# Feed-forward 1: two conditioning sums per turn instead of three groups, the output gate's group in the last turns, and mixer 1's transfers and cast moved around the loop

## What is computed

```python
def swiglu(x, w_gate, w_up, w_down):
    return (jax.nn.silu(x @ w_gate) * (x @ w_up)) @ w_down      # feed-forward 1: 1024 -> 2816 -> 1024

# block 2, the conditioning of the layer:
mod  = jnp.split(jax.nn.silu(c)     @ w_mod[l] + b_mod[l], N_MOD, axis=-1)   # six parts of 1024
modc = jnp.split(jax.nn.silu(c_ctx) @ w_mod[l] + b_mod[l], N_MOD, axis=-1)
```

## Time and profile before

| | |
|---|---|
| median of 3 runs | 1234.78 us |
| lowest, highest | 1228.0, 1242.36 us |
| the profiled execution, its own time | 1236.44 us |
| its span in the trace | 1234.8 us |
| granted TensorE clock, mean share of full | 0.988 |
| busy: PE, DVE, ACT, POOL | 1182.5, 840.1, 633.5, 554.2 us |

### The profile page before, as it was taken

How to read it: one execution, slowest core, us unless ns; L and a number is a source line. 1 busy time by engine, 2 the same in 40 slices (tenths; PEclk the granted TensorE clock), 3 DMA queues, 4 the chain that set the end, 5 groups by cost and what they waited for, 6 DMA issues and landing times.

```text
span 1234.8 us, 24412 instructions
## 1 busy us (share of the span) xinstructions
PE 1182.5 (96%) x9128; PEld 1109.5 (90%) x9128; DVE 840.1 (68%) x1133; ACT 633.5 (51%) x1014; POOL 554.2 (45%) x287
## 2 busy tenths in 40 slices
PE   6999998999999999999999999997999999999998
PEld 6999998987788999999999888886877899999998
DVE  6798985955986577777554852688745696655555
ACT  5434445525762454454445546467426635655553
POOL 0355646832555433443435645468630383232331
PEclk9999998999999999999989999999999999999999
DMA  8777774443334557788614333232323354656563
GB/s 314 234 274 280 268 233 152 138 135 118 105 105 137 170 188 256 276 287 288 190 48 153 114 100 130 86 104 85 103 69 104 92 181 137 188 188 190 188 193 107
DMA packets 58096, 207.04 MB, mean 168 GB/s; under 512 B 6576, under 2 KB 8240, under 8 KB 57776
## 3 DMA queue, kind: packets, MB, share of 16 engines
q1 hardware_dynamic: 49824, 177.23, 43.9%
q0 software_dynamic: 6912, 25.17, 5.7%
q10 hardware_dynamic: 1296, 3.74, 0.9%
HBM read 205.07 MB, written 1.05 MB: 167 GB/s over the span
## 4 chain that ended last, share of the span: by engine, by line
PE 62%; DVE 19%; issue 6%; ACT 5%; POOL 4%; DMA 3%; DVEq 0%; SPq 0%; POOLq 0%; ACTq 0%
PE psum L639 17%; PE psum L640 17%; PE psum L641 16%; DVE parts L2160 4%; DMA low<-stream 3%; POOL own_parts L2907 2%; POOL high L2990 2%; DVE high L2191 1%; PE psum L931 1%; PE psum L650 1%; PE psum L652 1%; ACT parts L1498 1%; PE psum L651 1%; PE psum L778 1%; ACT parts L1567 1%
## 5 line engine op out<-in xcount | busy, mean ns | idle before, releaser
L639 PE MATMUL psum<-parts 128*128 128x256 f32 x1584 | 442.8, 280 | 20.0 <-DVE parts L2160 10.0
L640 PE MATMUL psum<-parts 128*128 128x256 f32 x1584 | 445.5, 281 | 0.0
L641 PE MATMUL psum<-parts 128*128 128x256 f32 x1584 | 441.7, 279 | 0.0
L2915 POOL TENSOR_TENSOR parts<-low,parts 128x1024 fp32r<-128x1024 f32 x60 | 169.9, 2832 | 337.8 <-ACT parts L1498 337.8
L639 PEld LDWEIGHTS psum<-parts 128*128 128x128 f32 x1584 | 299.5, 189 | 23.3 <-issue 18.0
L640 PEld LDWEIGHTS psum<-parts 128*128 128x128 f32 x1584 | 299.5, 189 | 0.0
L641 PEld LDWEIGHTS psum<-parts 128*128 128x128 f32 x1584 | 299.4, 189 | 0.0
L1498 ACT ACTIVATE parts<-low 128x1024 fp32r<-128x1024 f32 x198 | 205.4, 1054 | 124.2 <-DMA low<-stream 123.4
L2907 POOL TENSOR_TENSOR own_parts<-low,parts 128x1024 fp32r<-128x1024 f32 x75 | 184.0, 2465 | 161.2 <-ACT parts L1567 161.1
L2160 DVE TENSOR_TENSOR parts<-low,parts 128x1024 fp32r<-128x1024 f32 x138 | 179.0, 1331 | 22.0 <-ACT parts L1498 21.3
L640 PE MATMUL psum<-u_parts,parts 128*128 128x256 f32 (+1 forms) x560 | 164.0, 293 | 0.0
(11 more groups left out here) (377 smaller groups left out, 2083.8 us busy)
## 6 DMA issues: line engine op xcount, KB each, us to landing
low<-stream SPq DMA_DIRECT2D x334, 512.0 KB, 3.5
high<-conditioning POOLq DMA_DIRECT2D x48, 512.0 KB, 5.2
high<-wuq ACTq DMA_DIRECT2D x1, 1152.0 KB, 11.4
low<-x SPq DMA_DIRECT2D x4, 256.0 KB, 5.9
high<-ctx ACTq DMA_DIRECT2D x1, 1024.0 KB, 6.5
out<-low SPq DMA_DIRECT2D x8, 128.0 KB, 1.8
low<-cst ACTq DMA_DIRECT2D x1, 850.5 KB, 5.6
low<-vec ACTq DMA_DIRECT2D x1, 157.5 KB, 5.8
```

The lines of the kernel that those rows point to most:

```text
L639: pe.matmul(out, w_hi[:, cols_], x_hi, start=start, stop=False, **kw)
L640: pe.matmul(out, w_hi[:, cols_], x_lo, start=False, stop=False, **kw)
L641: return pe.matmul(out, w_lo[:, cols_], x_hi, start=False, stop=stop, **kw)
L2915: pool.tensor_tensor(ring_lo[k][:, j % RING, :], ring[:, t % RING, :], ring_hi[:, j % RING, :], ALU.subtract).then_inc(S("lower_ready_2"), 1)
```

## The change

- `COND_TURN[0]` falls from 5 to 4: the loop of feed-forward 1 sums groups 0 and 1 only, each for `c` and `c_ctx`: two sums in par 0, two in par 1. POOL loads two tiles in each turn, no longer three.
- The eight sums of group 2 (`gate_sums`, m = 0 to 7) come in the ninth turn, three per par, and two more between chunk 20 and chunk 21. Each stands behind hidden's lower part and, in the ninth turn, ahead of the two `lower` of its par. Their tiles go in turn through all three places, by `gate_sum_place`: m=0 to place 2 (loaded ahead of the loop), 1 to 0, 2 to 1, 3 to 2, and so on.
- POOL issues the loads of m=1 and m=2 in the eighth turn behind its `lower` of each par, m=3, 4, 5 in the ninth turn behind `lower` of par 0 (tile 62), m=6 and 7 behind that of par 1 (tile 65); each waits for the sum that frees its place.
- The first tiles of groups 0 and 1 and of m=0 are no longer loaded at once, but behind POOL's `lower` of tiles 8 (group 0) and 11 (group 1, m=0).
- ACT's five transfers move from before the norm's root to behind the two written-out chunks (behind `upper` of tile 11), ahead of the loop.
- DVE's wait for tables and the cast move behind feed-forward 1.
- The second feed-forward keeps its order; its tile counts follow from `COND_LOADS`.

Constants and the place of each tile:

```diff
-COND_TURN = (5, 3)
+COND_TURN = (4, 3)
 COND_FROM = (5, 5 + DC * 5 + 3)
-COND_DONE = tuple(a + DC * b for a, b in zip(COND_FROM, COND_TURN))
+COND_DONE = (5 + DC * 5, COND_FROM[1] + DC * 3)
+COND_TAIL = COND_FROM[0] + DC * 4
+COND_LOADS = (DC + 3, DC + 2, 3)
+def gate_sum_place(m):
+    g = (m + 2) % 3
+    return g, (DC, DC, 0)[g] + (m - (1, 2, 0)[g]) // 3 + 1
```

ACT:

```diff
+            def mixer_1_transfers():
+                act.dma_start(cst[:, P:NCST], dram["cst"][:, P:NCST]).then_inc(S("tables_loaded"), 16)
+                act.dma_start(lam_p, dram["lam"].partition_broadcast(P)).then_inc(S("tables_loaded"), 16)
+                act.dma_start(pos_i, dram["pos"].partition_broadcast(P)).then_inc(S("tables_loaded"), 16)
+                act.dma_start(wuq, dram["wuq"]).then_inc(S("small_weights"), 16)
+                act.dma_start(A1("wkr", 8), dram["wkr"]).then_inc(S("small_weights"), 16)
...
                     upper(k, 8 + 3 * par)
+                if k == 0:
+                    mixer_1_transfers()
                 with act.Fori(0, DC) as i:
...
             uppers(0, 2, RING)
-            act.dma_start(cst[:, P:NCST], dram["cst"][:, P:NCST]).then_inc(S("tables_loaded"), 16)
...
             take_root("ffn1_pre", D)
```

DVE:

```diff
-                    for g in ((0,), (1, 2))[par]:
+                    for g in (((0,), (1,)) if k == 0 else ((0,), (1, 2)))[par]:
...
+                def gate_sums(first, last):
+                    for m in range(first, last):
+                        g, load = gate_sum_place(m)
+                        dve.wait_ge(S(f"cond_tile{g}"), 16 * load)
+                        dve.wait_ge(S("cond_steps"), COND_TAIL + m)
+                        dve.scalar_tensor_tensor(out=cond_sums[2], in0=cond_places[g], scalar=small[:, 2 * m:2 * m + 1],
+                                                 in1=cond_sums[2], op0=ALU.mult, op1=ALU.add).then_inc(S("cond_steps"), 1)
...
-                    turn(DC, lambda i, par: None)
+                    turn(DC, (lambda i, par: gate_sums(3 * par, 3 * par + 3)) if k == 0 else (lambda i, par: None))
...
                     lower_hidden(k, par, FC * k + FC - 2 + par)
+                    if k == 0 and par == 0:
+                        gate_sums(6, 8)
...
+            dve.wait_ge(S("cond_ready"), 1)
+            ffn(0)
             dve.wait_ge(S("tables_loaded"), 48)
             link(dve.tensor_copy(posf, pos_i))
-            dve.wait_ge(S("cond_ready"), 1)
-            ffn(0)
```

POOL:

```diff
-                after = (2, 4, 5) if k == 0 else (1, 2, 3)
-                if k < 2:
+                after = (2, 4) if k == 0 else (1, 2, 3)
+                def gate_tile(m):
+                    g, load = gate_sum_place(m)
+                    pool.dma_start(cond_places[g], dram["conditioning"][3 * m + 2]).then_inc(S(f"cond_tile{g}"), 16)
+                def first_tile(g):
+                    pool.dma_start(cond_places[g], dram["conditioning"][3 * DC * k + g]).then_inc(S(f"cond_tile{g}"), 16)
+                if k == 1:
                     for g in range(3):
+                        first_tile(g)
                 for par in range(2):
                     lower(k, 8 + 3 * par)
+                    if k == 0:
+                        if par == 0:
+                            first_tile(0)
+                        else:
+                            first_tile(1)
+                            gate_tile(0)
...
                     for i in (DC - 1, DC):
                         for par in range(2):
                             lower(k, 14 + 3 * par, i)
+                            if k == 0 and i < DC:
+                                pool.wait_ge(S("cond_steps"), COND_TAIL - 2 + 2 * par)
+                                gate_tile(1 + par)
+                            elif k == 0:
+                                for m in ((3, 4, 5), (6, 7))[par]:
+                                    pool.wait_ge(S("cond_steps"), COND_TAIL + m - 2)
+                                    gate_tile(m)
```

More of the change, by code:

```diff
@@ L2185, in condition @@
                     beside(i, par)
-                    for g in ((0,), (1, 2))[par]:
-                        dve.wait_ge(S(f"cond_tile{g}"), i * 16 + (16 * DC * k + 16))
+                    for g in (((0,), (1,)) if k == 0 else ((0,), (1, 2)))[par]:
+                        dve.wait_ge(S(f"cond_tile{g}"), i * 16 + (16 * COND_LOADS[g] * k + 16))
                         dve.wait_ge(S("cond_steps"), i * COND_TURN[k] + COND_FROM[k])
@@ L2918, in feed_forward @@
             def feed_forward(k):
-                after = (2, 4, 5) if k == 0 else (1, 2, 3)
-                if k < 2:
+                after = (2, 4) if k == 0 else (1, 2, 3)
[5 more added lines that the diff above has]
+                if k == 1:
                     for g in range(3):
-                        pool.dma_start(cond_places[g], dram["conditioning"][3 * DC * k + g]).then_inc(S(f"cond_tile{g}"), 16)
+                        first_tile(g)
                 for par in range(2):
                     lower(k, 8 + 3 * par)
+                    if k == 0:
[4 more added lines that the diff above has]
+                            gate_tile(0)
                 if k < 2:
```

## The result

The changed kernel is slower: 1246.96 us in the median of 11 runs (1242.56 to 1255.2), the kernel before 1234.82 in as many beside it (1228.0 to 1242.36). The ratio is 1.0100, with a 95% interval of 1.0076 to 1.0125: some 12 us, where 2.8 us less were forecast. The profiled execution took 1249.6 us, of which 1247.6 are span.

A forecast was written before the change was run, and what follows sets the result against it. It took PE, busy 96% of the span, as the bound, with DVE pacing feed-forward 1's loop. 1234.8 - 2.7 (early part) - 4.8 (loop) + 4.7 (tail) = 1232.0 us, range 1225 to 1241.

The forecast's parts named there:

- Cast, and the first two gaps: Start of feed-forward 1: moving cast and transfers shrinks PE's gaps near 25 and 36 us, winning 1.4 and 1.8 us.
- The flood's new place: Transfers and first tile loads moved to some 34 to 46 us: a new cost of 0.5 us, from nothing to 1.8.
- The loop: Feed-forward 1's loop: one sum less brings DVE's turn from 17.42 to 16.22 us, PE sets the pace, 4.8 us won.
- The argument that feed-forward 2 has nearly as much DVE work: Said against the rival that a second 2.2 us collision per turn keeps the loop at 17.4 us; 1236.8 us, chance 0.10.
- The tail: Last two and a half turns of feed-forward 1: eight sums and their loads cost 4.7 us, between 3.5 and 5.9.
- The three gaps: New PE gaps in the tail, before up(21), down(20) and down(21): 3.5 to 6 us together, the last most certain.
- the lower clock of down(21): Rival: PE's clock falls in the tail's gaps, 48 matmuls at 0.1 us more, 4.8 us; 1236.8 us, chance 0.05.
- The floor of 2.0 us: End of the tail: even with the fastest landing, 3.9 us, PE loses at least 2.0 us before down(21).
- late loads: Rival: three tail loads at once land in 10 us rather than 4.6, about 9.5 to 10 us lost; 1237.3, chance 0.15.
- The range's upper end: Top of the median's range: cases lie between 1229.3 and 1237.3 us, and a median moves by some 4 us by itself.

The follow-up runs named there:

- e1: Kernel before with ACT's five transfers behind tile 11's upper part and the cast behind feed-forward 1, sums and loads as before; 1237.07 us, ratio 1.0024.
- e7: Kernel before with the cast behind feed-forward 1 and ACT's five transfers in the ninth turn, five sums per turn; 1234.19 us, ratio 0.9986.
- e8: Kernel before with only the wait for tables and the cast moved behind feed-forward 1; 1236.33 us, ratio 1.0019.
- e9: Kernel before with the cast behind feed-forward 1 and ACT's transfers inside the loop, five sums per turn; 1233.70 us, ratio 0.9981.
- e10: Changed kernel without the gate group's eight sums and loads, ACT's transfers inside the loop; 1233.13 us, ratio 0.9976 to the kernel before.
- e11: Changed kernel, whole, with only ACT's transfers moved inside the loop; 1245.23 us, ratio 1.0092 to the kernel before.
- e5: Changed kernel where POOL begins its subtractions for mixer 1's first weights only when all conditioning sums are done; 1249.95 us, ratio 1.0089 to the kernel before.
- e4: Changed kernel where all eight gate sums read the first tile and the other seven are not loaded; 1240.77 us, ratio 1.0048 to the kernel before.
- e6: Changed kernel with the last two gate sums behind the last chunk's product and lower part; 1247.22 us, ratio 1.0083 to the kernel before.
- e13: Changed kernel with the gate tiles' loads kept but without the eight sums; 1238.38 us, ratio 1.0023 to the kernel before.

## Why the prediction was wrong, point by point

- *Cast, and the first two gaps:* right. The first product ran at 22.18 (22.0 forecast), 3.2 us were won (3.2 before the flood's cost).
- *The flood's new place:* wrong, the second largest miss. The step put down 0.5 us, with 1.8 as its end; the trace has 5.6, 4.0 of gap and 1.6 of lower clock. It had the landing right (10.2, measured 10.8), and it looked at each tile's own way to PE. What it left out is ACT's order: the silu of one chunk stands behind the upper part of a tile of a later one, so a tile that PE wants only later holds up a hidden part that PE wants now. The early part as a whole thus lost 2.4 instead of winning 2.7.
- *The loop:* the size was near, 3.8 us for 4.8, in these two executions; the reason was wrong. "DVE sets the pace of this loop" was read from one execution that ran in the pattern of collisions. e1, e7 and e8 run five sums at PE's pace or within 1% of it, and e9 against e10 gives the fifth sum 0.6 us, within the noise. The 2.2 us of collision in the earlier trace rows were taken as a fixed part of DVE's turn; the traces tie the slow pace to them. (The argument that feed-forward 2 has nearly as much DVE work was weak: by the earlier trace rows it has 12.5 us per turn, where 14.4 are left here.)
- *The tail:* the step that failed most. The three gaps that it named came where it said, before up(21), down(20) and down(21), and two more. The sum was 4.7 us, at most 5.9; the trace has 13.9, and e11 against e10 gives 12.1. Missing were, first, the collisions: the text allowed one, of tile 62; there were four, of 8.5 us together, two of them with POOL's subtractions for mixer 1, which were not in the working at all. Then the lower clock of down(21), 2.5 us, which had a chance of 0.05. The floor of 2.0 us for the last gap was far too low for this trace (6.8); it is no floor either, since e5 has 1.6 there.
- *The rival "late loads"* (10 us lost) comes nearest in size, but its condition did not hold: it wanted a landing of 10 us in the tail, and the seven loads took 5.1, close to the forecast's 4.6. DVE waited 3.3 us for them in the changed kernel. They matter even so: in e4, without them, 6 of the 12 us of the median come back; the other half stays.
- *The range's upper end*, 1241, came from adding up only one rival at a time. The flood, the tail's collisions and the clock all came together. That in the tail each late link put the next one beside a POOL instruction or a standing PE is how I read the traces; no run varies it alone.

Open: how often executions of the kernel before run in the pattern of collisions. Its median cannot be split, so the loop's share in the 12 us is known from traces alone. Nor was a version found that beats the kernel before beyond the noise.

## What to carry over

An in-order engine's slack must be counted for the instruction that is wanted first, with everything that stands ahead of it in its queue, work for later tiles among it. Before a gap in one trace is put down to an edit, look whether it lies ahead of what the edit touches: e5 and e6 show one that does. Where two engines block each other, the length of an instruction in one trace is no property of it: ask what it is with the other engine at each possible place, and count for each instruction moved what runs beside it there. Work is not free in a stretch where its engine idles, when that stretch ends in a chain of short round trips with nothing to spare.

## What the runs showed of the hardware

- A sum with two SBUF inputs on DVE takes 1.22 us alone, 3.34 with a POOL subtraction begun before it; a lower part of 256 columns goes from 0.43 to 2.62. The forecast had such prices for DVE's `lower` and for hidden's lower part (1.49), not for the sums.
- PE did nothing in gaps of 2.33 (e11), 2.56 (e1), 3.04 (e8), 4.09 and 6.80 us (changed kernel), and its granted clock fell to 0.50 in the gap or within 1.4 us behind it; behind 2.07 (e4), 2.12 (changed kernel) and 2.46 us (e13) it stayed at full. The length of the gap alone does not decide: 2.33 us went one way, 2.46 the other. The price was 16 slow matmuls (1.6 us) behind a gap of 4.09 us in the changed kernel and 2.4 us behind one of the same length in e4; behind 6.80 it was a whole tile (2.5 us).
- The same loop, with the same instructions, ran at 17.4 us per turn in the kernel before and at 16.6 in e8, which differs from it only ahead of the loop and behind it; e9 changed from 16.6 to 17.4 within one execution.
